# Order of the first attention's steps: table addition and maxima before the filler's eviction on VectorE, four turns before the filler on TensorE

## What is computed

```python
def one_row(r):
    ...
    s_lat = jnp.einsum("bqhd,bkhd->bhqk", qb, kb, preferred_element_type=jnp.float32) * scale + bias
    s_lat = jnp.where(band_mask, s_lat, -jnp.inf)
    s_ctx = jnp.einsum("bqhd,bkhd->bhqk", qb, k_ctx, preferred_element_type=jnp.float32) * scale
    p = jax.nn.softmax(jnp.concatenate([s_lat, s_ctx], -1), -1).astype(v.dtype)
    n_lat = kh * GRID_W
    return (jnp.einsum("bhqk,bkhd->bqhd", p[..., :n_lat], vb)
            + jnp.einsum("bhqk,bkhd->bqhd", p[..., n_lat:], v_ctx))
```

## Time and profile before

| what | value |
|---|---|
| time, median of 3 runs | 1650.33 us (1649.56 to 1651.39) |
| time of the profiled execution | 1652.48 us |
| its span in the trace | 1650.7 us |
| mean granted clock of TensorE | 0.996 |
| the attention's steps in the span | 113.5 to 204.9 us |

### The profile page before, as it was taken

One profiled execution on the slowest core, in us unless ns is written; L12 is line 12 of the kernel. 1 busy time (PEld: TensorE's weight loads), 2 busy tenths in 40 slices (PEclk: granted clock), 3 DMA queues, 4 the chain that ended last, 5 costly groups with the idle time before them and its releaser, 6 DMA issues.

```text
span 1650.7 us, 22123 instructions
## 1 busy us (share of the span) xinstructions
PE 1600.7 (97%) x9282; PEld 1152.6 (70%) x9283; DVE 858.1 (52%) x1193; ACT 609.9 (37%) x822; POOL 27.7 (2%) x48
## 2 busy tenths in 40 slices
PE   6999999999999999999998999999999999999998
PEld 4965567875444444444447877799997877799997
DVE  3749766643222222222227774855446685765444
ACT  2414453321111111111123666454343566544431
POOL 0200000000000000000000000000000000000000
PEclk9999999999999999999999999999999999999999
DMA  9976864667999999999983435456445543565540
GB/s 357 250 228 235 304 226 141 242 245 316 421 421 421 421 421 421 421 421 421 421 320 139 167 130 192 157 177 216 154 161 183 191 148 110 203 200 183 177 156 26
DMA packets 148434, 418.57 MB, mean 254 GB/s; under 512 B 6976, under 2 KB 55248, under 8 KB 123312
## 3 DMA queue, kind: packets, MB, share of 16 engines
q1 hardware_dynamic: 126048, 271.19, 45.3%
q10 hardware_dynamic: 17568, 127.93, 18.6%
q0 software_dynamic: 4720, 18.03, 4.0%
HBM read 416.07 MB, written 2.95 MB: 254 GB/s over the span
## 4 chain that ended last, share of the span: by engine, by line
PE 90%; DVE 5%; ACT 1%; issue 1%; DMA 1%; SPq 1%; DVEq 0%
PE bank L971 22%; PE bank L1342 14%; PE bank L1636 12%; PE bank L1353 7%; PE bank L1586 6%; PE bank L1324 4%; PE bank L1363 4%; PE bank L986 3%; PE bank L922 3%; PE bank L1160 3%; PE bank L1607 3%; PE bank L953 1%; DVE ring_low L2554 1%; DMA weight_ring<-in_w_ada 1%; PE bank L1287 1%
## 5 line engine op out<-in xcount | busy, mean ns | idle before, releaser
L2554 DVE TENSOR_TENSOR ring_low<-weight_ring,high_ring 128x2048 fp32r<-128x2048 f32 x92 | 208.1, 2288 | 52.1 <-ACT high_ring L1869 51.8
L1342 PE MATMUL bank<-weight_ring,arena 128*64 128x512 f32 x800 | 232.1, 592 | 0.7 <-DVE arena L2474 0.7
L971 PE MATMUL bank<-high_ring,split 128*128 128x512 f32 x608 | 196.2, 396 | 0.9 <-DVE split L2561 0.9
L971 PE MATMUL bank<-ring_low,split 128*128 128x512 f32 x464 | 181.3, 398 | 0.0
L1342 PEld LDWEIGHTS bank<-weight_ring,arena 128*64 128x64 f32 x800 | 74.5, 137 | 150.2 <-issue 150.2
L1869 ACT ACTIVATE high_ring<-weight_ring 128x2048 fp32r<-128x2048 f32 x92 | 172.2, 1906 | 10.5 <-PE bank L971 5.9
L1636 PE MATMUL bank<-split,ring_low 128*128 128x256 f32 x576 | 162.6, 282 | 0.0
L1636 PE MATMUL bank<-split,high_ring 128*128 128x256 f32 x832 | 148.9, 280 | 0.0
L971 PEld LDWEIGHTS bank<-high_ring,split 128*128 128x128 f32 x608 | 114.1, 188 | 31.9 <-issue 3.2
L1636 PEld LDWEIGHTS bank<-split,high_ring 128*128 128x128 f32 x832 | 128.7, 189 | 0.7
L1353 PE MATMUL bank<-weight_ring,arena 128*64 128x512 f32 x400 | 120.5, 598 | 0.6 <-DVE arena L2474 0.6
(11 more groups left out here) (335 smaller groups left out, 2832.9 us busy)
## 6 DMA issues: line engine op xcount, KB each, us to landing
weight_ring<-in_w_in SPq DMA_DIRECT2D x62, 1024.0 KB, 7.8
weight_ring<-in_w_e_gate SPq DMA_DIRECT2D x49, 1024.0 KB, 9.2
weight_ring<-in_w_e_up ACTq DMA_DIRECT2D x46, 1024.0 KB, 13.5
weight_ring<-in_w_e_down ACTq DMA_DIRECT2D x46, 1024.0 KB, 12.7
weight_ring<-in_w_ada SPq DMA_DIRECT2D x24, 1024.0 KB, 11.7
weight_ring<-in_w_ffn_gate SPq DMA_DIRECT2D x22, 1024.0 KB, 5.5
weight_ring<-in_w_ffn_up SPq DMA_DIRECT2D x22, 1024.0 KB, 8.0
weight_ring<-in_w_ffn_down SPq DMA_DIRECT2D x22, 1024.0 KB, 5.7
```

What stands on the lines that cost most here:

```text
L971: last = mm(bank(key)[:, :], left[a_][:, n, t * P:(t + 1) * P], wv[b_][:, j, :], start=(n == 0 and i == 0), stop=(n == kts * len(units_) - ...
L1342: last = mm(hidden_bank[side * CAP:(side + 1) * CAP, :].rearrange("p (j n) -> p j n", n=FF), xgT[:, p // 2 % 2, kt, at:at + CAP], hidden_u ...
L2554: V.tensor_tensor(lower(key), ring[:, units.place[key][0], :], upper(key, layer), ALU.subtract)\
```

## The change

On TensorE, in steps 1 to 7, all four turns stand ahead of the whole filler; before, the first quarter of the filler stood between the second and the third turn. On VectorE, in steps 1 to 7, the eviction of the filler of the step before stands behind the negated maxima and ahead of the modulation products; before, it stood first, ahead of the table addition. In step 8, which has no scores, the eviction stays where it was. No instruction is added or taken away, and the lists of ScalarE, SP and POOL stay as they are.

```diff
@@ TensorE
                 if s < NA_QUADS:
                     na_scores(s)
                 if s:
-                    na_turn(s - 1, 0)
-                    na_turn(s - 1, 1)
-                if s < NA_QUADS:
-                    na_fill(s, 0)
-                if s:
-                    na_turn(s - 1, 2)
-                    na_turn(s - 1, 3)
-                for q in range(1, 4):
+                    for i in range(4):
+                        na_turn(s - 1, i)
+                for q in range(4):
                     if s < NA_QUADS:
                         na_fill(s, q)
                 if s:
@@ VectorE
             for s in range(NA_QUADS + 1):
-                if s:
+                def filled():
                     name, n, t = fill[s - 1]
                     biased_out((name, n, t), (v_ if name == "v" else u_)[:, t, n * CHUNK:(n + 1) * CHUNK])
+
+                if s == NA_QUADS:
+                    filled()
                 if s < NA_QUADS:
                     t, g = divmod(s, 4)
                     for i in range(4):
@@
                     step(V.tensor_reduce(most, quad_bank, AX_X, ALU.max))
                     settle()
                     V.tensor_scalar(most, most, -1.0, None, ALU.mult).then_inc(sem("na_max"), 1)
+                    if s:
+                        filled()
                     for kt in range(KT):
                         ada_product(4 + s, ada[s], kt)
```

## The result

The changed kernel took 1674.60 us (median of 5 runs, 1673.69 to 1683.68), the kernel before in the same rounds 1651.12 us (5 runs, 1649.56 to 1652.44). The ratio is 1.0151 with a 95% interval of 1.014 to 1.0163: 23.5 us slower. The profiled execution happened to be the slowest of the five, 1683.68 us with a span of 1681.9 and a mean granted clock of 0.988; the four others had 0.993 to 0.995. So the profile must be read with two things apart: what the order costs in every run, and what the clock adds in this one.

A forecast was written before the change was run, and what follows sets the result against it. TensorE, busy for 97% of the span, was taken as the bound. Ordinary steps 18.7, step 1 2.9 and the clock 5.2 summed to 26.8 us on 1650.3: 1677.1 us, range 1670.5 to 1684.

The forecast's parts named there:

- Which wait decides: First attention: the filler's first product on TensorE waits until VectorE's eviction of the previous filler empties its single bank.
- An ordinary step: Each of steps 2 to 7 of the first attention takes 13.79 us instead of 10.68, 3.11 more.
- Step 1: First attention: filler starts 3.74 us later, less 0.87 of turns no longer behind it, so 2.9 us more.
- The turns: Steps 1 to 7: the second pair waits for ScalarE's copies, 0.50 us a step, hidden by the late eviction.
- What waits behind: Modulation products, loads and bias rows get more room and nothing later absorbs the delay: no cost, 1 us either way.
- The clock: Seven new TensorE pauses, one in two followed by a clock fall: 3.5 falls of 1.5 us, 5.2 us.
- rival 1: TensorE's clock stays up or falls once: 21.6 or 23.3 us slower, 1671.9 to 1673.6; chance 0.30.
- the forecast's own 1675 to 1684: Main case: the clock falls in two to seven steps, 21.6 + 3 to 21.6 + 11.9 us more; chance 0.64.
- The price of a fall: 3.4 us at half speed, 1.7 of work less what lies in a pause; taken as 1.5 us.
- Rival 2: VectorE's chain sets the step and the change shortens it: 2.6 us gained, 1647.7; chance 0.02.
- The Trainium skill's rule: A long pause between matmul bursts lowers the clock; its limit lies between both pause lengths here, so one fall, not 3.5.

The follow-up runs named there:

- TensorE kept busy: The changed kernel with products of no use behind the fourth turn, four in step 1, two in each of steps 2 to 7: 1671.78 us, ratio 1.0131.
- VectorE's part alone: The changed kernel with TensorE put back in its old order, only the eviction still late on VectorE: 1694.79 us, ratio 1.0254.
- third profile: The changed kernel executed a third time without edit: 1673.85 us for the profiled execution, 1680.45 for one more, ratio 1.0158.
- second profile: The changed kernel executed again without edit: 1674.95 us (5 runs), ratio 1.0143.
- the kernel with two banks: The kernel before, both engines in the old order, with every second filler in bank 7 and the attention's output in bank 0: 1649.53 us, ratio 0.9989.

## Why the prediction was right, and where it was off

The predicted time was 1677.1 us with a range of 1670.5 to 1684; measured were 1674.6. The mechanism was right, and its part of the sum, 21.6 us, came out at 21.0; the clock's part was twice too large. Point by point:

- *Which wait decides.* Right: the filler's single bank. A second bank takes 18.3 of the loop's 21.0 us away, the eviction two instructions earlier 17.3 (88.44 for the loop), and the rest is mostly the turns.
- *An ordinary step*, 3.11 more: measured 3.04 to 3.06 (13.72 to 13.74). The eviction starts at +4.92 where I had +4.97; this is nearly all of the difference.
- *Step 1*, 2.9 more: measured 2.78 with TensorE kept busy (15.39 against 12.61).
- *The turns*, 0.50 a step, hidden by the eviction: 0.58 when alone, and hidden in the change, as the single pause behind them ends with VectorE's semaphore.
- *What waits behind.* Right: modulation products end at +11.6 (159.96 + 5.55 - 153.92), VectorE waits before every addition of steps 2 to 7 (3.38 to 6.45 in the first profile), and the part behind the loop is the same within 2 us.
- *The clock*, 3.5 falls of 1.5 us: this is the term that was mis-sized. "One in two followed by a fall" was taken from two pauses of over 2 us in one profile, 2.04 with a fall and 3.39 without, and it made one kind of two. Here they are two kinds: the 3.9 us pause of step 1 had a fall in every profile, the 2.2 us pauses in 4 of 18. Two profiled runs of three, 1674.07 and 1673.85 us, have the fall of step 1 alone, worth 1.7 to 3.1, not 5.2; that the other runs near 1674 are like them is inferred from their times. So the fixed 21.0 plus about 2.5 gives the 23.5 measured, and the case that most runs show is my rival 1 with one fall (1673.6), to which I gave 0.30; only three runs of twelve lie clearly inside the forecast's own 1675 to 1684. The range holds the median by its fixed part, since 1650.3 + 21.0 is 1671.3 already; it says nothing for the 3.5 falls, and that the first profile had five was chance. The price of a fall was low as well: 2.6 and 3.1 in step 1 of the first two profiles, as the low stretch there lasts 6.8 us, not 3.4; the third had 3.4 and 1.7.
- *Rival 2* (VectorE's chain is the pace) fell: the exponentials start at +5.04 (158.96), where it was +5.16, and no pause of TensorE in steps 1 to 7 is put down to them.

The Trainium skill's rule that I set against the rows ("TensorE: Matmul & The Clock Gate", section "Why this matters for your kernels") came out better than my reading of them: it puts the limit between the two kinds of pause, and the runs agree with it for step 1 (a fall in all three profiles) and for VectorE's part alone (7 of 7). They don't quite agree for the ordinary pauses, 4 of 18 of which had a fall in spite of it, and the 3.39 us of the kernel before without one stand against it on the other side.

## What to carry to other kernels

Before moving an eviction later on its engine, ask who writes the same bank next and when: with a single buffer the whole delay lands on the writer, past the point where its other work runs out (here 3.4 us into the step), however full the evicting engine was before (VectorE, 94% of a step). A second buffer, or a place two instructions earlier, avoids nearly all of it. Where TensorE must pause as long as here in step 1 or with VectorE's part alone (3.65 us and more), add the clock's fall to the price, or put in work. Before work is moved into a pause, ask what else starts behind it: here two quarters of a projection ahead of a few small transposes held up a chain with 5.7 us to spare.

## What the runs showed of the hardware

The length of a pause of TensorE does not by itself tell whether the clock falls. Between the last transposes and the filler, pauses of 3.65 to 3.9 us came with the lower clock in 9 of 9 over four profiles, and 5.33 once in one; 2.2 us in 4 of 18; pauses of 0.4 to 0.5 us, with products of no use before them, in none of 7. Elsewhere in the kernel before, 2.04 us had a fall and 3.39 had none. The lower level began inside the pause or up to 1.4 us behind its end. The stretch at the lower level lasted 3.4 us (the four ordinary falls, and step 1 of the third profile) or 6.8 us (step 1 of the first two profiles, and all seven steps of VectorE's part alone), and cost 1.5 to 3.1 us of TensorE's work: half of what lay outside the pause. In step 1 of the second profile 5.2 of the 6.8 us lay outside, and the step was 2.6 longer than with TensorE kept busy.

A fall needs no pause at all: in the kernel before the clock went down just ahead of 222, while TensorE was at work without a gap, behind four products with only 4 rows (L1193), and the next twelve took 4.55 us, where the same twelve took 3.07 in the kernel with two banks.

Whether the 2.2 us pauses fall or not differs between executions of the same kernel with pauses that agree to 0.03 us: the twelve runs of the change scatter over 10 us, while 22 runs of the kernel before, beside the second five of them, scatter over 6 (1648.2 to 1654.5). What decides it within one execution was not tried.
